# Ending a mixture-of-experts step: the list of further blocks made early, the branches put ahead of the last scatter, and TensorE summing four of nine tiles

## The chip, the cores and the metric

The kernel runs on one core of one Trainium2 chip. Its time is the device time of one execution in microseconds (us). Three runs of the kernel before took 1218.40, 1216.89 and 1221.19 us; the median is 1218.4.

## The reference, cut to what matters

The program is one inference step of a decoder layer with 1024 prompt tokens and 8 sample tokens, 1032 rows of 1024 float32 values in nine tiles: eight of 128 rows, and one of 8. The change touches only the end of the layer, the experts' sum and the final norm:

```python
# each token has one of 4 groups, and in it the best 2 of 8 experts (32 experts in all)
def expert_block(xb, e):
    return (jax.nn.silu(xb @ w_gate[e]) * (xb @ w_up[e])) @ w_down[e]
out = segment_sum(gate_s[:, None] * ybuf[dest], tok_s, num_segments=T)   # two rows a token
h = h + out
y = h * rsqrt(mean(h * h, axis=-1) + EPS) * norm_final
```

So for each token the end computes x + gate0 * y0 + gate1 * y1, and then its RMS norm with the gain.

## The kernel before, in words

Up to the router all goes on as it will after the change: projections, attention, the output projection, the residual sum `xres` in SBUF (nine tiles of 128 x 1024), and the router. The router gives every (token, choice) pair a slot in its expert's block of 96 rows.

**The expert loop** (`for b in range(NE + 1)`, on every engine) runs over 32 experts. SyncE loads 6 MB of weights for each. ScalarE rounds each weight to its upper part (L1316), and VectorE subtracts to get the lower part (L1869, two halves to each of gate, up and down). TensorE makes three products for each pair of tiles (L1032 to L1034, L1063 to L1065). GpSimd fetches the 96 token rows of an expert by an indirect DMA (L1985). It sends the 96 result rows by another (L1990, `send`) to `y_rows` in DRAM: the first choices of all tokens lie in its first half, and the second choices in the other. The result rows have one SBUF buffer, `ysb`, which ScalarE fills (`copy_y`, L1331). Before it fills it for expert b-1, it waits until the rows of expert b-2 are sent (`act.wait_ge(first.sent, 16 * (b - 1))`). The last expert, 31, has its own place for the upper parts of `w_down`.

Experts are taken in such an order that the first choices are complete four experts before the end. So SyncE reads their eight full tiles back while the last experts are computed (`load_y(t, 0, ...)`, L637), and the ninth after the first add.

**The list of further blocks** (`list_further`, L1785 to L1796, VectorE). An expert can have over 96 rows. How many further blocks there are, and of which experts, is worked out from the counts by ten short instructions. With the inputs here there are none. The program must still read the number and branch, on each of the five engines. The list is made after VectorE's last work of the expert loop, and `listed` tells the others.

**The end.** VectorE adds the first choices to all nine tiles (`add_choice(t, 0)`, L1925, nine instructions in a row). Then TensorE, VectorE, ScalarE and GpSimd wait until the last rows are out of their hands: VectorE, ScalarE and GpSimd for all scatters (`first.sent`), TensorE for the last copy. Each reads the number and branches, and GpSimd signals `all_sent`. SyncE waits for `all_sent`, loads the second choices tile by tile (L637), and VectorE does for each tile: the second add (L1925), which ScalarE squares and sums (L1400) and takes the root of (L1403); the reciprocal (L1964); and the closing product (L1967) into one of three output tiles, which SyncE writes out (L685). VectorE's order is add 0, add 1, close 0, add 2, close 1, and so on.

Every engine takes its instructions in order. SyncE's DMAs go in one queue, GpSimd's in another.

## Time and profile before

| what | before |
|---|---|
| median of three runs | 1218.4 us |
| profiled execution | 1217.44 us |
| its span | 1215.4 us |
| TensorE busy | 1148.7 us (95%) |
| VectorE busy | 854.0 us (70%) |
| ScalarE busy | 667.0 us (55%) |
| GpSimd busy | 110.8 us (9%) |
| DMA | 295.12 MB, mean 243 GB/s |

The profile is of one execution. Busy shares are means over the whole span; the change touches its last 50 us and a few microseconds at the start of the expert loop, so the stretches and the chain of waits there say more than the shares. PE is TensorE's products, DVE is VectorE, ACT ScalarE, POOL GpSimd and SP SyncE; SPq is SyncE's queue of DMA issues. The granted TensorE clock of 1.00 is 2.4 GHz, and 0.50 is 1.2 GHz.

### The profile page before, as it was taken

The numbers are of one execution on the slowest core, as the hardware profiler recorded it, in microseconds if no ns is written. First come the engines' busy times: TensorE is split into PE (matmuls) and PEld (weight loads), VectorE is DVE, ScalarE is ACT, GpSimd is POOL, SyncE is SP. The second block draws the span as 40 slices with busy tenths as digits, with TensorE's granted clock in tenths as the row PEclk, the third lists the DMA queues.
The fourth block names the chain that finished last, engine by engine and source line by source line (L and its number), as shares of the span: only waits on it lengthen the run. The fifth ranks groups of instructions, "written<-read, shape, count | busy, mean of one in ns | idle before, by whom it ended". The sixth has DMA issues, their size and how long they took to land.

```text
span 1215.4 us, 17163 instructions
## 1 busy us (share of the span) xinstructions
PE 1148.7 (95%) x6818; PEld 902.1 (74%) x6818; DVE 854.0 (70%) x1213; ACT 667.0 (55%) x831; POOL 110.8 (9%) x130
## 2 busy tenths in 40 slices
PE   7999999999899989999799999999999999999950
PEld 6999999999677747888467777777777777777740
DVE  6315343321677746888788889889888988888877
ACT  7212231111368752332477777777777777777724
POOL 1012210021000000000011111111111111111110
PEclk9999999999999999999899999999999999999985
DMA  8125556141211032111799999999999999999857
GB/s 258 41 80 167 186 185 209 37 138 53 73 51 42 1 132 116 70 70 70 261 395 392 397 395 400 388 388 393 395 389 387 400 387 385 394 395 390 312 215 275
DMA packets 77714, 295.12 MB, mean 243 GB/s; under 512 B 8649, under 2 KB 33353, under 8 KB 52930
## 3 DMA queue, kind: packets, MB, share of 16 engines
q1 hardware_dynamic: 65954, 258.27, 55.6%
q0 software_dynamic: 11680, 35.75, 8.9%
q8 instruction: 55, 0.90, 0.3%
q14 instruction: 25, 0.20, 0.1%
HBM read 268.58 MB, written 33.77 MB: 249 GB/s over the span
## 4 chain that ended last, share of the span: by engine, by line
PE 91%; DVE 3%; ACT 2%; DMA 2%; issue 1%; POOLq 0%; SPq 0%; ACTq 0%; DVEq 0%
PE psum L1034 10%; PE psum L1032 10%; PE psum L1033 10%; PE psum L751 8%; PE psum L753 7%; PE psum L752 7%; PE psum L1063 5%; PE psum L1065 5%; PE psum L1064 5%; PE psum L907 3%; PE psum L829 3%; PE psum L909 3%; PE psum L844 3%; PE psum L908 3%; PE psum L867 2%; PE psum L1022 2%
## 5 line engine op out<-in xcount | busy, mean ns | idle before, releaser
L751 PE MATMUL psum<-h_hi,w_hi 128*128 128x344 f32 x576 | 186.0, 323 | 3.0 <-DVE h_lo L1483 3.0
L753 PE MATMUL psum<-h_hi,w_lo 128*128 128x344 f32 x576 | 184.2, 320 | 0.0
L752 PE MATMUL psum<-h_lo,w_hi 128*128 128x344 f32 x576 | 184.1, 320 | 0.0
L1869 DVE TENSOR_TENSOR w_down_lo<-w_down,w_down_hi 128x2048 fp32r<-128x2048 f32 x62 | 139.4, 2288 | 44.8 <-ACT w_down_hi L1316 44.7
L1869 DVE TENSOR_TENSOR w_gate_lo<-w_gate,w_gate_hi 128x2048 fp32r<-128x2048 f32 x64 | 144.3, 2289 | 23.1 <-ACT w_gate_hi L1316 21.8
L1869 DVE TENSOR_TENSOR w_up_lo<-w_up,w_up_hi 128x2048 fp32r<-128x2048 f32 x64 | 143.7, 2287 | 2.7
L1316 ACT CAST w_gate_hi<-w_gate 128x2048 fp32r<-128x2048 f32 x64 | 119.9, 1915 | 4.4 <-DMA w_gate<-in_w_gate 4.2
L1316 ACT CAST w_up_hi<-w_up 128x2048 fp32r<-128x2048 f32 x64 | 119.3, 1917 | 0.7 <-DMA w_up<-in_w_up 0.6
L1316 ACT CAST w_down_hi<-w_down 128x2048 fp32r<-128x2048 f32 x62 | 115.7, 1907 | 0.7 <-DMA w_down<-in_w_down 0.6
L751 PEld LDWEIGHTS psum<-h_hi,w_hi 128*128 128x128 f32 x576 | 108.3, 188 | 5.4 <-DVE h_lo L1483 3.9
L753 PEld LDWEIGHTS psum<-h_hi,w_lo 128*128 128x128 f32 x576 | 108.4, 188 | 0.0
L752 PEld LDWEIGHTS psum<-h_lo,w_hi 128*128 128x128 f32 x576 | 108.3, 188 | 0.0
L1432 DVE TENSOR_TENSOR w_lo<-w_raw,w_hi 128x1024 fp32r<-128x1024 f32 x23 | 28.1, 1223 | 110.4 <-ACT w_hi L1148 110.4
L1032 PE MATMUL psum<-w_gate_hi,xT_hi 128*96 128x512 f32 x256 | 101.8, 398 | 3.2 <-issue 3.2
L1032 PE MATMUL psum<-w_up_hi,xT_hi 128*96 128x512 f32 x256 | 102.4, 400 | 0.0
L1034 PE MATMUL psum<-w_gate_hi,xT_lo 128*96 128x512 f32 x256 | 101.8, 398 | 0.0
L1033 PE MATMUL psum<-w_gate_lo,xT_hi 128*96 128x512 f32 x256 | 101.4, 396 | 0.0
L1034 PE MATMUL psum<-w_up_hi,xT_lo 128*96 128x512 f32 x256 | 101.1, 395 | 0.0
L1033 PE MATMUL psum<-w_up_lo,xT_hi 128*96 128x512 f32 x256 | 100.7, 393 | 0.0
L1985 POOL DMA_INDIRECT x_rows<-h_rows,gidx x32 | 43.8, 1370 | 612.6 <-DVE gidx L1768 310.1
L1063 PE MATMUL psum<-w_down_hi,hT_hi 128*96 128x512 f32 x248 | 99.4, 401 | 0.0
L1065 PE MATMUL psum<-w_down_hi,hT_lo 128*96 128x512 f32 x248 | 97.7, 394 | 0.0
(252 smaller groups left out, 2065.9 us busy)
## 6 DMA issues: line engine op xcount, KB each, us to landing
w_gate<-in_w_gate SPq DMA_DIRECT2D x64, 1024.0 KB, 15.4
w_up<-in_w_up SPq DMA_DIRECT2D x64, 1024.0 KB, 14.3
w_down<-in_w_down SPq DMA_DIRECT2D x64, 1024.0 KB, 14.1
w_raw<-in_w_in SPq DMA_DIRECT2D x24, 512.0 KB, 4.4
y_tile<-y_rows SPq DMA_DIRECT2D x16, 512.0 KB, 10.4
kv<-in_cache_k POOLq DMA_DIRECT2D x24, 256.0 KB, 4.7
kv<-in_cache_v POOLq DMA_DIRECT2D x24, 256.0 KB, 4.7
x_tile<-in_x_prompt SPq DMA_DIRECT2D x8, 512.0 KB, 4.7
```

Of the source, the lines that this page charges most:

```text
L751: mm(ps[:, 0:TC], wh[:, k, :], h_hi[:, k, cols], start=(k == 0), stop=False)
L752: mm(ps[:, 0:TC], wh[:, k, :], h_lo[:, k, cols], start=False, stop=False)
L753: ins = mm(ps[:, 0:TC], wl[:, k, :], h_hi[:, k, cols], start=False, stop=(k == KD - 1))
L1032: mm(bank(b)[0:SLOTS, :], xT_hi[:, k, :], hi[:, k, :], start=(k == 0), stop=False)
L1033: mm(bank(b)[0:SLOTS, :], xT_hi[:, k, :], lo[:, k, :], start=False, stop=False)
L1034: ins = mm(bank(b)[0:SLOTS, :], xT_lo[:, k, :], hi[:, k, :], start=False, stop=(k == KD - 1))
L1063: mm(out, hT_hi[:, m, :], wd_hi[:, m, cols], start=(m == 0), stop=False)
L1064: mm(out, hT_hi[:, m, :], wd_lo[s][:, m, cols], start=False, stop=False)
L1065: ins = mm(out, hT_lo[:, m, :], wd_hi[:, m, cols], start=False, stop=(m == DE // P - 1))
L1316: nc.scalar.copy(dst[:, part, :], src[:, part, :]).then_inc(ready, 1)
L1869: vec.tensor_tensor(dst[:, part, :], src[:, part, :], hi[:, part, :].bitcast(F32), ALU.subtract).then_inc(split, 1)
L1985: gp.indirect_dma_start(xg, None, h2_d[:, :], bass.IndirectOffsetOnAxis(ap=idx, axis=0)).then_inc(f.rows_in, 16)
```

## The change

**The list** is made after `finish_gates`, ahead of VectorE's loop over the experts. Its small tiles move behind the expert buffers in SBUF. Its two wide intermediates, which had lain in SBUF, now lie in bank 7 of PSUM, and the comparison with 22 block numbers is made in two halves of 11, since a bank holds 512 values in a row. The semaphores `listed` and `early_added` become one, `end_step`: 1 is the list, 2 to 10 are the nine early adds, and 11 to 14 are the four diagonal matrices.

**The branches** of TensorE, ScalarE and VectorE no longer wait for the last scatter or copy ahead of the reading of the number; that wait stands in the branch that is not taken. SyncE now waits for `first.sent` itself and not for GpSimd's `all_sent`. GpSimd keeps its order.

**TensorE's tiles.** For tiles 0 to 3 VectorE makes a 128 x 128 diagonal matrix of the second gates after its early adds. TensorE runs six filler products (`keep_clock`) behind its last expert product. It then multiplies the identity by `xres` of each of the four tiles into two PSUM banks each (eight products), and, when the second choices of a tile have landed, the tile's diagonal by them onto the same banks. `mixed` counts these tiles. ScalarE squares and VectorE closes them from PSUM. Tiles 4 to 8 are added by VectorE as before.

**The order** of the tiles at the end, for the loads, the squares, the closing products and the writes, is 0, 4, 1, 5, 2, 6, 3, 7, 8. VectorE adds tiles 4 and 5 first, then closes tile 0, then 4, adds 6, closes 1 and 5, adds 7, closes 2 and 6, adds 8, and closes 3, 7 and 8.

```diff
@@ -217,11 +217,10 @@
         over = Pack(WEI + 3 * 16384, WEI + 4 * 16384)
-        r_ob, r_inc = (over(f"re{i}", [NE]) for i in range(2))
-        r_mul = over("r_mul", [MORE])
-        r_gt = over("r_gt", [NE, MORE])
-        r_cmp = over("r_cmp", [OVER, NE])
-        r_list = over("r_list", [OVER])
+        listing = Pack(TMP + 16384 + 8 * NE, END)
+        r_ob, r_inc = (listing(f"re{i}", [NE]) for i in range(2))
+        r_mul = listing("r_mul", [MORE])
+        r_list = listing("r_list", [OVER])
         o_mul = over("o_mul", [MORE])
@@ -245,6 +244,9 @@
         gfin = at("gfin", unit(5), [D])
+        MIXED = 4
+        gate_diag = [at(f"gate_diag{k}", unit(5) + 4096 + 4 * P * k, [P]) for k in range(MIXED)]
+        fin_order = [0, 4, 1, 5, 2, 6, 3, 7, 8]
         r_count = at("r_count", TMP + 16384, [NE])
@@ -643,11 +645,11 @@
             sp.dma_start(gfin, a["norm_final"].partition_broadcast(P)).then_inc(gfin_in, 16)
-            sp.wait_ge(early_added, 1)
+            sp.wait_ge(end_step, 2)
             load_y(NY, 0, y_in[0])
-            sp.wait_ge(early_added, NT)
+            sp.wait_ge(end_step, NT + 1)
             sp.wait_ge(first.y_done, NE)
-            sp.wait_ge(listed, 1)
+            sp.wait_ge(end_step, 1)
             more = sp.value_load(oexp[0:1, OVER:OVER + 1], min_val=0, max_val=OVER)
@@ -673,16 +675,16 @@
-            sp.wait_ge(all_sent, 1)
-            for t in range(NY):
+            sp.wait_ge(first.sent, 16 * NE)
+            for t in fin_order[0:NY]:
                 load_y(t, 1, y_in[t])
-            for t in range(NT):
-                if t == 0:
-                    sp.wait_ge(fin_res, 1)
+            for i, t in enumerate(fin_order):
+                if i == 0:
+                    sp.wait_ge(mixed, 1)
                     load_y(NY, 1, y_in[0])
-                sp.wait_ge(fin_out, t + 1)
+                sp.wait_ge(fin_out, i + 1)
                 dst = a["y_prompt"][P * t:P * (t + 1), :] if t < NQ else a["y_sample"]
-                sp.dma_start(dst, ot[t % NO][0:rows(t), :]).then_inc(out_sent[t % NO], 16)
+                sp.dma_start(dst, ot[i % NO][0:rows(t), :]).then_inc(out_sent[i % NO], 16)
             for o in out_sent:
@@ -1088,10 +1090,11 @@
                         down(first, (b - 1) % 2, b - 1, wd_hi_end, hT_hi_end, hT_lo_end)
-            pe.wait_ge(first.y_out, NE)
-            pe.wait_ge(listed, 1)
+            keep_clock(6, bank(0), 512)
+            pe.wait_ge(end_step, 1)
             more = pe.value_load(oexp[0:1, OVER:OVER + 1], min_val=0, max_val=OVER)
             with pe.If(more > 0):
+                pe.wait_ge(first.y_out, NE)
                 place_further()
@@ -1102,6 +1105,20 @@
                     pe.wait_ge(first.y_out, n + 1)
+                pe.wait_ge(back_added, NT)
+            pe.wait_ge(first.y_out, NE)
+            pe.wait_ge(end_step, NT + 1)
+            for k in range(MIXED):
+                for half in range(2):
+                    cols = slice(half * 512, (half + 1) * 512)
+                    mm(bank(2 * k + half), ident, xres[:, k, cols], start=True, stop=False)
+            pe.wait_ge(end_step, NT + 1 + MIXED)
+            for k in range(MIXED):
+                pe.wait_ge(y_in[k], 48 if k == 0 else 32)
+                for half in range(2):
+                    cols = slice(half * 512, (half + 1) * 512)
+                    ins = mm(bank(2 * k + half), gate_diag[k], yt[k][:, cols], start=False, stop=True)
+                ins.then_inc(mixed, 1)
@@ -1376,10 +1393,10 @@
                     upper_down(b)
-            act.wait_ge(first.sent, 16 * NE)
-            act.wait_ge(listed, 1)
+            act.wait_ge(end_step, 1)
             more = act.value_load(oexp[0:1, OVER:OVER + 1], min_val=0, max_val=OVER)
             with act.If(more > 0):
+                act.wait_ge(first.sent, 16 * NE)
                 with act.Fori(0, more, 1) as o:
@@ -1393,13 +1410,18 @@
-            for t in range(NT):
+            for i, t in enumerate(fin_order):
                 w = rows(t)
-                act.wait_ge(fin_res, t + 1)
-                c = t % 2
-                step(nc.scalar.activation(fjunk[0:w, :], xres[0:w, t, :], ACT.Square, accum_out=ssq_f[0:w, c:c + 1]))
-                if t >= 2:
-                    act.wait_ge(fin_out, t - 1)
+                c = i % 2
+                if t < MIXED:
+                    act.wait_ge(mixed, t + 1)
+                    total = bank(2 * t, 2)
+                else:
+                    act.wait_ge(fin_res, t - MIXED + 1)
+                    total = xres[0:w, t, :]
+                step(nc.scalar.activation(fjunk[0:w, :], total, ACT.Square, accum_out=ssq_f[0:w, c:c + 1]))
+                if i >= 2:
+                    act.wait_ge(fin_out, i - 1)
                 nc.scalar.activation(std_f[0:w, c:c + 1], ssq_f[0:w, c:c + 1], ACT.Sqrt, bias=eps[0:w, :],
@@ -1783,17 +1805,21 @@
                 step(vec.tensor_scalar(r_mul, ramp[:, 1:MORE + 1], float(SLOTS), None, ALU.mult))
+                r_gt = bank(7)[:, 0:NE * MORE].rearrange("p (e j) -> p e j", e=NE)
                 step(vec.tensor_tensor(r_gt, r_count.unsqueeze(2).broadcast_to([P, NE, MORE]),
...
                 vec.tensor_copy(oexp[0:1, OVER:OVER + 1], r_inc[0:1, NE - 1:NE])
-                step(vec.tensor_tensor(r_cmp[0:1], r_inc[0:1].unsqueeze(1).broadcast_to([1, OVER, NE]),
-                                       ramp[0:1, 0:OVER].unsqueeze(2).broadcast_to([1, OVER, NE]), ALU.is_le))
-                step(vec.tensor_reduce(r_list[0:1, :], r_cmp[0:1], X, ALU.add))
+                for lo, hi in ((0, OVER // 2), (OVER // 2, OVER)):
+                    n = hi - lo
+                    r_cmp = bank(7)[0:1, 0:n * NE].rearrange("p (o e) -> p o e", o=n)
+                    step(vec.tensor_tensor(r_cmp, r_inc[0:1].unsqueeze(1).broadcast_to([1, n, NE]),
+                                           ramp[0:1, lo:hi].unsqueeze(2).broadcast_to([1, n, NE]), ALU.is_le))
+                    step(vec.tensor_reduce(r_list[0:1, lo:hi], r_cmp, X, ALU.add))
                 step(vec.tensor_scalar(r_list[0:1, :], r_list[0:1, :], float(NE - 1), None, ALU.min))
-                vec.tensor_copy(oexp[0:1, 0:OVER], r_list[0:1, :]).then_inc(listed, 1)
+                vec.tensor_copy(oexp[0:1, 0:OVER], r_list[0:1, :]).then_inc(end_step, 1)
@@ -1899,6 +1925,7 @@
             finish_gates()
+            list_further()
             for b in range(NE + 1):
@@ -1916,8 +1943,6 @@
                     lower_down(first, b % 2, b)
-                if b == NE - 1:
-                    list_further()
@@ -1927,10 +1952,13 @@
                 dve.wait_ge(y_in[t % NY], 16 * (t // NY) + 16)
-                add_choice(t, 0).then_inc(early_added, 1)
-            dve.wait_ge(first.sent, 16 * NE)
+                add_choice(t, 0).then_inc(end_step, 1)
+            for k in range(MIXED):
+                vec.tensor_scalar(gate_diag[k], ident, gates[:, 1, k:k + 1], None, ALU.mult).then_inc(end_step, 1)
+            dve.wait_ge(end_step, 1)
             more = dve.value_load(oexp[0:1, OVER:OVER + 1], min_val=0, max_val=OVER)
             with dve.If(more > 0):
+                dve.wait_ge(first.sent, 16 * NE)
                 table_further()
@@ -1957,23 +1985,26 @@
-            def finish(t):
+            def finish(i):
+                t = fin_order[i]
                 w = rows(t)
-                c = t % 2
-                dve.wait_ge(fin_std, t + 1)
+                c = i % 2
+                total = bank(2 * t, 2) if t < MIXED else xres[0:w, t, :]
+                dve.wait_ge(fin_std, i + 1)
                 step(vec.reciprocal(rst_f[0:w, c:c + 1], std_f[0:w, c:c + 1]))
-                if t >= NO:
-                    dve.wait_ge(out_sent[t % NO], 16 * (t // NO))
-                vec.scalar_tensor_tensor(out=ot[t % NO][0:w, :], in0=xres[0:w, t, :], scalar=rst_f[0:w, c:c + 1],
+                if i >= NO:
+                    dve.wait_ge(out_sent[i % NO], 16 * (i // NO))
+                vec.scalar_tensor_tensor(out=ot[i % NO][0:w, :], in0=total, scalar=rst_f[0:w, c:c + 1],
                                          in1=gfin[0:w, :], op0=ALU.mult, op1=ALU.mult).then_inc(fin_out, 1)
...
-            dve.wait_ge(early_added, NT)
+            dve.wait_ge(end_step, NT + 1)
             dve.wait_ge(gfin_in, 16)
-            add_experts(0)
-            for t in range(NT):
-                if t + 1 < NT:
-                    add_experts(t + 1)
-                finish(t)
+            add_experts(MIXED)
+            add_experts(MIXED + 1)
+            for i, t in enumerate(fin_order):
+                finish(i)
+                if t >= MIXED and t + 2 < NT:
+                    add_experts(t + 2)
@@ -2032,7 +2063,7 @@
             pool.wait_ge(first.sent, 16 * NE)
-            pool.wait_ge(listed, 1)
+            pool.wait_ge(end_step, 1)
             more = pool.value_load(oexp[0:1, OVER:OVER + 1], min_val=0, max_val=OVER)
```

## Rows read from the trace of the kernel before

**Rows 1.** Busy time by stretch: PE, PEld, DVE, ACT, POOL, PEclk, DMA share, GB/s.

```profile
620.00:1150.00 530.00, 530.00 (x2521) 377.75 (x2520) 466.65 (x302) 412.18 (x331) 68.59 (x58) 1.00 1.00 389
1174.00:1184.00 10.00, 0.00 (x0) 0.00 (x0) 5.89 (x5) 1.01 (x1) 3.74 (x2) 0.70 0.10 29
1174.00:1215.40 41.40, 0.00 (x0) 0.00 (x0) 29.11 (x32) 15.17 (x29) 3.74 (x2) 0.55 0.56 211
```

**Rows 2.** Chain of waits at the end: start us, us, what.

```profile
1174.04 1.02 ACT y_rows L1331
...
1175.84 6.31 DMA y_rows<-y_rows,sidx
...
1183.30 4.28 DMA y_tile<-y_rows
...
1192.01 1.28 DVE out_tile L1967
...
1194.60 1.28 DVE out_tile L1967
...
1211.73 1.27 DVE out_tile L1967
```

**Rows 3.** Order of time, ScalarE, first square: start us, us, idle before in brackets.

```profile
1189.02 1.06 ACT L1400 ACTIVATE fjunk<-xres 128x1024 f32<-128x1024 f32 x1 [13.97 <-DVE xres L1925]
```

**Rows 4.** Order of time, VectorE: first experts, a late expert, the end.

```profile
613.73 4.49 DVE L1869 TENSOR_TENSOR w_gate_lo<-w_gate,w_gate_hi 128x2048 fp32r<-128x2048 f32 x2 [4.95 <-ACT w_gate_hi L1316]
...
1107.86 2.29 DVE L1869 TENSOR_TENSOR w_gate_lo<-w_gate,w_gate_hi 128x2048 fp32r<-128x2048 f32 x1 [0.50 <-ACT w_gate_hi L1316]
...
1165.28 0.16 DVE L1785 TENSOR_SCALAR r_mul<-cst 128x10 f32<-128x10 f32 x1
...
1169.06 10.83 DVE L1925 SCALAR_TENSOR_TENSOR xres<-y_tile,gates,xres 128x1024 f32<-128x1024 f32 x9
...
1178.63 1.27 DVE L1925 SCALAR_TENSOR_TENSOR xres<-y_tile,gates,xres 8x1024 f32<-8x1024 f32 x1
```

**Rows 5.** Order of time, TensorE: eight fillers, and the second expert's start.

```profile
590.21 7.11 PE L705 MATMUL psum<-cst 128*128 128x512 f32 x16
...
619.26 0.45 PE L1032 MATMUL psum<-w_gate_hi,xT_hi 128*96 128x512 f32 x1 [1.76 <-issue]
```

**Rows 6.** DMA issues from 1154.76, 1168.90, 1185.69, 1193.32: KB, us to landing.

```profile
y_tile<-y_rows SPq DMA_DIRECT2D x1, 512.0 KB, 14.6
...
y_rows<-y_rows,sidx POOLq DMA_INDIRECT x1, 3.6
...
y_tile<-y_rows SPq DMA_DIRECT2D x1, 512.0 KB, 6.5
...
out_y_prompt<-out_tile SPq DMA_DIRECT2D x1, 512.0 KB, 5.6
```

**Rows 7.** Order of time, SyncE's queue: start us, us of the issue.

```profile
1154.76 0.47 SPq L637 DMA_DIRECT2D y_tile<-y_rows  x1
...
1184.16 1.48 SPq L637 DMA_DIRECT2D y_tile<-y_rows  x1
...
1185.69 0.43 SPq L637 DMA_DIRECT2D y_tile<-y_rows  x1
```

**Rows 8.** Order of time, GpSimd: a late fetch and the last two scatters.

```profile
1109.05 1.89 POOL L1985 DMA_INDIRECT x_rows<-h_rows,gidx  x1 [9.53 <-PE psum L1022]
...
1168.90 0.92 POOL L1990 DMA_INDIRECT y_rows<-y_rows,sidx  x1 [16.29 <-ACT y_rows L1331]
1175.84 3.65 POOL L1990 DMA_INDIRECT y_rows<-y_rows,sidx  x1 [6.02 <-ACT y_rows L1331]
```

**Rows 9.** Order of time, VectorE: SBUF inputs, one PSUM input, one-source pair.

```profile
479.92 0.68 DVE L1589 TENSOR_TENSOR a_lo<-qT,a_hi 128x512 fp32r<-128x512 f32 x1
...
502.30 0.75 DVE L1619 SCALAR_TENSOR_TENSOR xres<-psum,stat,xres 128x512 f32<-128x512 f32 x1 [1.09 <-PE psum L909]
...
514.56 0.57 DVE L1704 TENSOR_SCALAR hot_slot<-cst,r_rank_of 128x96 f32<-128x96 f32 x2
```

More of the change, by code:

```diff
@@ L395, in program @@
         res_out = sem("res_out")
-        listed = sem("listed")
         y_cleared = sem("y_cleared")
-        early_added = sem("early_added")
+        end_step = sem("end_step")
         back_in = sem("back_in")
@@ L402, in program @@
         fin_res = sem("fin_res")
+        mixed = sem("mixed")
         fin_std = sem("fin_std")
```

## The prediction

> **What bounds the kernel now.** I read first the busy time by stretch, to see which stage the change can touch. In the expert loop TensorE is busy all 530 us of the stretch from 620 to 1150 and the clock is at its upper level, 2.4 GHz [rows 1]. Nothing that VectorE, ScalarE or a queue saves there shortens the run, so long as it does not make TensorE wait. From 1174 on TensorE does nothing: in 41 us the end is set by others [rows 1].
>
> Then the chain of waits over these 41 us [rows 2] (a DMA's piece ends at its landing). The last product ends at 1174.0, ScalarE copies it until 1175.06, GpSimd starts the last scatter at 1175.84, it has landed at 1182.15, GpSimd then takes over a microsecond to read the count of further blocks, pass the branch and signal, and SyncE issues the loads of the second-choice rows at 1183.30. The first tile lands at 1187.58. From there the chain is VectorE's: nine adds and nine closing products, until 1213.00. ScalarE's wait before the first square, 14 us, is a wait for this chain and not a bound [rows 3].
>
> Third, VectorE's own order of time around the last experts. The list takes it from 1165.28 to 1169.06, and the nine early adds from 1169.06 to 1179.89, at a pitch of (10.83 - 1.27) / 8 = 1.195 us [rows 4]. None of this is on the path, but it is what GpSimd meets, and this decides the case.
>
> **The list, moved to the start of the experts.** It takes 3.78 us now. The two long instructions of 704 elements become four of 352, and the wide operands lie in PSUM. Four short ones cost what two long ones cost plus two starts, which I put at 0.15 each, and I allow nothing more for PSUM: 4.1 us. VectorE is idle for 4.95 us just there, from 608.78 to 613.73, waiting for ScalarE's first half of the next gate weights [rows 4]. So it is hidden with 0.85 us to spare. The cover is thin, because the split of these weights is followed by that of the token rows, and TensorE sat 1.76 us until 619.26, where those rows are ready [rows 5]: what the list takes over 4.95 us is added to the run. Lower end 0. For the upper end let every one of its wide instructions take twice its time, some 2.6 us more, which gives 1.8 us. I take 0. Behind the last expert VectorE is free 3.78 us earlier, and its adds start at 1165.28. The first-choice tiles are no bar: the last of eight, issued at 1154.76, landed 14.6 us later, at 1169.4, and is used by the eighth add at 1173.6 [rows 6, 7].
>
> **What the earlier adds do to the scatters.** An index row is read from SBUF by GpSimd before it makes the descriptors. In the loop a fetch that was asked for at 1109.05, in the middle of a split by VectorE with both inputs in SBUF, ended at 1110.94, which is 0.79 us after the split's end at 1110.15; a scatter that meets no such work takes 0.92 [rows 4, 8]. The last scatter was asked for at 1175.84, in the sixth early add. It ended at 1179.49, and this is 0.79 us after the end of the eighth add (the ninth started at 1178.63, and two neighbours overlap by 0.07). So it stood through two borders between adds, was let in behind the last add over 128 partitions, and the ninth, over 8 partitions, did not hold it.
>
> The scatter before it, of expert 30, was asked for at 1168.90, while the list's short instructions ran, and took 0.92 [rows 8]. After the change it is asked for at the same time in the fourth of nine adds that follow one another from 1165.28. By the row just read it waits until the eighth add ends, 1165.28 + 7 x 1.195 + 1.27 = 1174.9, and its descriptors are out at 1175.7. It landed 3.6 us after its start, thus 2.7 after its end [rows 6], so now at 1178.4. ScalarE's last copy waits for this landing, since the rows' buffer is single: it starts at 1178.45 instead of 1174.04 and ends at 1179.5. GpSimd starts 0.78 us later as before (1175.06 to 1175.84), at 1180.25, with VectorE idle by then, and the last scatter lands at 1180.25 + 3.6 = 1183.85, against 1182.15. **Term: +1.7 us.**
>
> The Trainium skill, "SBUF — State Buffer", section "Who interferes with whom", says that a VectorE instruction with two SBUF inputs blocks a GpSimd one that reads SBUF, for the whole instruction, and that whichever starts first has the ports. The holding agrees with the trace, the release does not: by that rule the last scatter would have been let in at 1176.3 and not at 1178.70. What the rule would make of the change is the first rival.
>
> **The branch ahead of the last scatter.** SyncE now waits for the scatter itself, with count and branch behind it. GpSimd's 1183.30 - 1182.15 = 1.15 us leave the path [rows 2]; with 0.05 for the wake-up, **-1.1 us**. The loads are issued from 1183.9, and the first tile is there after the same 4.28 us, at 1188.2. The count is read by TensorE, VectorE, ScalarE and SyncE between 1174 and 1178, beside the wait for the scatter. GpSimd's branch comes behind it, where nobody waits for it.
>
> **TensorE's part.** A product of 512 columns in plain float32 took 7.11 / 8 = 0.89 us at the upper clock [rows 5]. Six fillers run from 1174.0 to 1179.3; eight products that bring the four tiles' sums into PSUM follow once the copy has ended, 1179.5 to 1186.6; then it waits for the first tile. Of the 10 us from 1174 the mean grant is 0.70 [rows 1]: 4 us at the upper level and 6 at half, so it held to about 1178, and a wait of 1.6 us should not lower it, and tile 0 is summed at 1188.2 + 1.8 = 1190.0. At half clock it would be 1191.8. ScalarE and VectorE then need 1192.01 - 1189.02 = 3.0 us to the first closing product (square, table load, root, reciprocal) [rows 2, 3]: ready at 1193.0.
>
> But VectorE has two adds in its queue ahead of that product, of tiles 4 and 5. Tile 5 is fourth in the load order. The fourth load was issued at 1185.69 and landed 6.5 us later, at 1192.2, which is 4.6 us behind the first [rows 6, 7]. So now it lands at 1192.8, its add ends at 1194.1, and the first closing product starts at 1194.2 instead of 1192.01. **Term: from the 0.6 us of a later first tile (1.7 - 1.1) to 2.2 us late, +1.6.** It hangs on SyncE's third load, which took 1.48 us to issue where the fourth took 0.43 [rows 7]. If that hitch goes, the term is 1.0 smaller; I keep it, as nothing in the change touches the loads.
>
> **The closing chain.** The pitch of add and product together was 1194.60 - 1192.01 = 2.59 us [rows 2], of the product alone 2.59 - 1.195 = 1.395. From the start of the first product on there were 20.99 us. Now there are five steps without and three with an add, and the last product: 5 x 1.395 + 3 x 2.59 + 1.28 = 16.0. Four products read PSUM instead of SBUF. For 512 columns 0.75 us stand against 0.68 with both inputs in SBUF [rows 9], so 4 x 0.08 = 0.3; lower end 0, upper end 0.6. **Term: 16.3 - 21.0 = -4.7 us.** ScalarE needs some 1.4 us a tile and keeps up. TensorE's tiles 1 to 3 are due long before their turn: even at half clock they would be ready by 1202.6, and the last is wanted at about 1206. Three output buffers: the first write landed 5.6 us after its issue, behind the last load [rows 6]; the fourth product starts 5.4 us after the first one starts, 4.1 after it ends. The last load now lands at 1198.2, and a write queued behind it about 1.3 later, 1199.5; the fourth product is due at 1199.6. It just fits; upper end 1.5 us.
>
> Sum: 1.7 - 1.1 + 1.6 - 4.7 = **-2.5 us**. The profiled execution took 1217.44 us with a span of 1215.4, and it becomes 1214.9. It was 1.0 us below the median of three runs, so for the median 1218.4 - 2.5 = **1215.9 us**. Its own range, by the ends above (hitch gone -1.0, list +1.8, writes +1.5, half clock +0.6, not all together), is 1214.6 to 1217.9.
>
> **Rivals.** (1) The scatter of expert 30 is let in at the next border of adds and lands before 1174. Then the copy stands at 1174.04, the last scatter is asked for at 1175.84, in the ninth add, which ends at 1176.1, is ready at 1176.9 at the latest, and lands at 1179.6. First tile at 1183.9, but TensorE's queue reaches 1186.4 with its fillers and eight products, tile 0 is summed at 1188.2, the first product starts at 1191.2 and the end is 1207.5: -5.5, **1212.9 us**. For it: the page's rule, and the hold over several adds is seen once only. Against it: that one row. (2) The hold lasts until VectorE's queue is empty. Four diagonals, at under 0.3 us each by a pair that took 0.57 [rows 9], follow the adds and end at 1177.3. Then the descriptors are out at 1178.1, the scatter lands at 1180.8, the last one at 1186.25, the first tile at 1190.6; TensorE, idle from 1179.3 to 1181.9 and again before the tile, drops to half clock, tile 0 is summed at 1194.2, the first product is at 1197.2 and the end at 1213.5: +0.5, **1218.9 us**. This is the slower side, and it decides from a release after 1177.4 or so. For it: the hold was over several instructions. Against it: the ninth add let GpSimd in. (3) The list outgrows its gap and TensorE waits at the second expert: -2.5 + 1.8, **1217.7 us**.
>
> **How the numbers follow.** Chances: forecast 0.66, (1) 0.20, (2) 0.08, (3) 0.06. A measurement of this kernel tells 0.3% from no change, which is 3.7 us, so faster means under 1214.7. Of the forecast's 0.66 about 0.11 lies below that (the hitch gone, or the scatter of the runs, 1216.9 to 1221.2), of (1) 0.18: 0.29. Slower, over 1222.1, needs (2) and a mishap more: 0.04. The range runs from (1) to just below (2), 1212.7 to 1218.4.
>
> **What would show it.** In the changed kernel's trace: the scatter of expert 30 lasting some 6.8 us instead of 0.92; ScalarE's last copy starting at its landing and not at the last product's end; the loads issued at the last scatter's landing, without GpSimd's memset between; VectorE waiting for tile 5 ahead of the first closing product; 16.3 us from there to the end. A scatter of expert 30 under 2 us makes me wrong towards (1). A split of the second expert's gate weights that starts later than 613.73 shows (3).

## The result: 6.8 us faster, outside the predicted range

The changed kernel took 1211.07 us (median of 6 runs, 1209.94 to 1214.16), the kernel before, beside it, 1217.88 us (1216.61 to 1222.5). The ratio is 0.9945, with an interval of 0.9926 to 0.9964. The forecast was 1215.9 with a range down to 1212.7: too little gain. The profiled executions are 1217.44 and 1210.50 us, and -6.94 us is what has to be explained.

I cut both at the request of the last scatter and call what follows, until the last closing product ends, the tail. The chain of waits at the end, changed kernel (start us, us, what):

```profile
1173.40 5.15 PE psum L707 x12
1178.55 6.87 PE psum L1114 x16
1185.42 1.73 PE psum L1120 x4
...
1187.17 1.11 ACT fjunk L1422 x2
...
1190.12 1.28 DVE out_tile L1997
...
1204.82 1.27 DVE out_tile L1997
```

The last two scatters, GpSimd's order of time (in brackets the idle time before):

```profile
1168.35 0.91 POOL L2021 DMA_INDIRECT y_rows<-y_rows,sidx  x1 [10.63 <-ACT y_rows L1348]
1175.29 1.16 POOL L2021 DMA_INDIRECT y_rows<-y_rows,sidx  x1 [6.03 <-ACT y_rows L1348]
```

The first load of a second-choice tile, SyncE's queue, and the DMA issue of 1175.29 with its us to landing:

```profile
1179.21 0.34 SPq L639 DMA_DIRECT2D y_tile<-y_rows  x1
```

```profile
y_rows<-y_rows,sidx POOLq DMA_INDIRECT x1, 3.9
```

| stage | before | after | change |
|---|---|---|---|
| until the last scatter's request | 1175.84 | 1175.29 | -0.55 |
| request to the first load's issue | 7.46 | 3.92 | -3.54 |
| issue to the first closing product | 8.71 | 10.91 | +2.20 |
| first closing product to the end of the last | 20.99 | 15.97 | -5.02 |

The sum is -6.91. The tail alone went from 37.17 to 30.80 us. The scatter of expert 30, the hinge of the forecast, took 0.91 and not 6.8 us: the copy was never late. The last scatter took 1.16 instead of 3.65 [rows 8]: it was asked for in the ninth add, the last of the row, and was out 0.87 us after that add's end. The chain before the first closing product changed hands: it is TensorE's queue (fillers until 1178.5, eight products until 1185.4, the sum of tile 0), not SyncE's loads. The busy time by stretch shows it (us, PE, PEld, DVE, ACT, POOL, PEclk, DMA share, GB/s), beside [rows 1]:

```profile
1174.00:1184.00 10.00, 10.00 (x25) 4.40 (x24) 2.49 (x6) 0.50 (x1) 1.25 (x2) 1.00 0.46 159
1184.00:1208.00 24.00, 8.82 (x20) 3.22 (x18) 18.41 (x23) 13.36 (x28) 0.00 (x0) 0.78 0.75 299
```

VectorE, changed kernel, order of time:

```profile
611.72 0.17 DVE L1822 CAST oexp<-r_list 1x22 int32<-1x22 f32 x1
611.81 4.48 DVE L1895 TENSOR_TENSOR w_gate_lo<-w_gate,w_gate_hi 128x2048 fp32r<-128x2048 f32 x2
...
1164.73 10.85 DVE L1950 SCALAR_TENSOR_TENSOR xres<-y_tile,gates,xres 128x1024 f32<-128x1024 f32 x9
...
1168.31 1.29 DVE L1950 SCALAR_TENSOR_TENSOR xres<-y_tile,gates,xres 128x1024 f32<-128x1024 f32 x1
...
1187.11 1.28 DVE L1950 SCALAR_TENSOR_TENSOR xres<-y_tile,gates,xres 128x1024 f32<-128x1024 f32 x1 [1.28 <-DMA y_tile<-y_rows]
1190.12 1.28 DVE L1997 SCALAR_TENSOR_TENSOR out_tile<-psum,stat,gfin 128x1024 f32<-128x1024 f32 x1
1191.51 1.28 DVE L1997 SCALAR_TENSOR_TENSOR out_tile<-xres,stat,gfin 128x1024 f32<-128x1024 f32 x1
```

The reader is to see three things. The fourth early add starts at 1168.31, and the scatter was asked for at 1168.35: 3.62 us after the row of adds began, within 0.04 us of a border between two of them. Tile 5's add started at 1187.11, when its load had landed, and was over 1.7 us before the first product. The last two lines show that a closing product costs 1.28 us from PSUM as from SBUF.

The early list did outgrow its gap in this execution, which is rival 3. It took 4.26 us, from 607.63 to 611.89, where 4.1 had been reckoned. ScalarE had its first half ready at about 608.69 + 1.9 = 610.6, and VectorE started the split at 611.81. TensorE then waited 2.93 us (1.76 before [rows 5]) and ran at half clock for a while:

```profile
608.69 3.70 ACT L1333 CAST w_gate_hi<-w_gate 128x2048 fp32r<-128x2048 f32 x2
```

```profile
617.32 0.71 PE L1034 MATMUL psum<-w_gate_hi,xT_hi 128*96 128x512 f32 x1 [2.93 <-issue]
```

```profile
617.00:620.40 3.40, 3.08 (x8) 2.07 (x9) 3.40 (x4) 3.40 (x3) 0.07 (x1) 0.50 1.00 418
```

The gap itself had shrunk. In the kernel before TensorE ran part of the first expert at half clock (0.51 from 601 to 608 us), in this execution it did not (1.00 there). Two variants of the kernel before that come below, b_shift1 and b_shift3, had 1.00 there as well, and left VectorE 2.90 and 2.87 us where [rows 4] has 4.95:

```profile
612.67 4.49 DVE L1869 TENSOR_TENSOR w_gate_lo<-w_gate,w_gate_hi 128x2048 fp32r<-128x2048 f32 x2 [2.90 <-ACT w_gate_hi L1316]
```

Of the eight profiles with the early list only this one and a_best, both with 1.00 there, overran the gap; the other six had 0.27 to 1.16 us to spare. The stages ahead of the tail move by microseconds from profile to profile: the last scatter was asked for between 1171.85 us (b_shift3) and 1177.63 (b_list_early), a_shift8 aside. So the tail is the sharper measure below, though each is read in a single profile. In the changed kernel and its three shifted variants it came out as 30.8 us four times.

### The profile page after: what moved, and what is told of

Its sections match the earlier page's. It is cut to its first block, busy times and chain, and to the rows that moved or that the text cites. A ratio compares the mean times of both kernels' runs of the same rounds, so it can differ in the third digit from the quotient of the medians.

```text
span 1208.4 us, 17253 instructions
## 1 busy us (share of the span) xinstructions
PE 1168.3 (97%) x6862; PEld 909.2 (75%) x6862; DVE 850.3 (70%) x1215; ACT 666.0 (55%) x831; POOL 112.8 (9%) x130
## 4 chain that ended last, share of the span: by engine, by line
PE 93%; ACT 3%; DVE 2%; issue 1%; DMA 1%; SPq 0%; ACTq 0%; DVEq 0%; POOLq 0%
PE psum L1036 10%; PE psum L1034 10%; PE psum L1035 10%; PE psum L753 8%; PE psum L755 7%; PE psum L754 7%; PE psum L1065 5%; PE psum L1067 5%; PE psum L1066 5%; PE psum L909 3%; PE psum L846 3%; PE psum L831 3%; PE psum L911 3%; PE psum L910 3%; PE psum L869 2%; PE psum L1024 2%
```

## The experiments

Two questions: why was the scatter of expert 30 not held, and what is each part of the change worth? Ratios are to the kernel before, run beside. Where only one execution was made, its time says little: beside b_gaps, b_shift10, a_shift8 and a_shift16 the kernel before was itself executed once, in 1214.77 us, and beside b_shift1, b_shift3 and b_ts2 its median was 1217.2. There the trace is what counts.

**Moving the adds against the scatter.** One to sixteen short stepped instructions go ahead of the row of early adds, in the changed kernel (N = 3, 8, 16) or the kernel before (N = 1, 3, 10):

```
+ for _ in range(N):
+     step(vec.memset(stat[:, 86:87], 0.0))
  for t in range(NT):
      dve.wait_ge(y_in[t % NY], 16 * (t // NY) + 16)
      add_choice(t, 0)...
```

> The changed kernel with three tiny VectorE instructions, each waited for, ahead of the nine early adds, so that the adds start some 0.5 us later. Theory H (hold): a scatter whose index read is asked for inside a row of back-to-back VectorE instructions over 128 partitions with two SBUF inputs waits until the row breaks, and the changed kernel escaped only because the request at 1168.35 fell on the border of the third and fourth add (1168.31). Moved by 0.5 us the request falls inside an add: the scatter of expert 30 lasts some 7 us in place of 0.91, ends 0.8 us after the eighth add, the last scatter lands about 4 us later, the closing chain starts 2 to 2.5 us later: 1213.4 us against 1211.1. Rival Q (the long scatter in the kernel before comes from the queue or the ring of descriptors, not from VectorE's adds): the scatter stays at 0.9 us and the time at 1211.1.

Measured: 1211.82 us (1210.55 to 1212.47), ratio 0.9958 (0.9943 to 0.9973), tail 30.8 us.

```profile
1170.32 1.24 POOL L2023 DMA_INDIRECT y_rows<-y_rows,sidx  x1 [10.10 <-ACT y_rows L1348]
1177.26 1.54 POOL L2023 DMA_INDIRECT y_rows<-y_rows,sidx  x1 [5.70 <-DVE xres L1950]
```

The row of adds began at 1167.10, so the scatter of expert 30 came in the middle of the third add, away from any border, and was out at 1171.56, 0.79 us after that add's end (1167.10 + 2 x 1.195 + 1.27 = 1170.76). It was let in at the next border. So the border at which it fell in the changed kernel was not the whole reason. The tail did not move with the longer scatters: TensorE's queue, which the first closing product waits for, does not depend on them.

> The changed kernel with sixteen tiny VectorE instructions ahead of the early adds, 1.9 us later, so that the scatter of expert 30 is asked for in the second add. Theory E: held until the eighth add ends, 8.8 us. Theory F: 4.0 us. Next border: 1.6 us.

Measured (one execution): 1211.65 us; the scatter of expert 30 in the second add, 1.67 us, the last in the eighth, 1.91 us, both let in at the next border. Tail 30.8 us.

> As a_shift16 with eight, 1.0 us later: the scatter of expert 30 is asked for 0.2 us into the third add. Theory E: 7.9 us. Theory F: 4.3 us. Next border: 1.85 us.

Measured (one execution): 1216.32 us, tail 30.8 us: the loss lies ahead of it. The scatters of experts 29, 30 and 31, and ScalarE's copy for expert 30:

```profile
1151.69 12.51 POOL L2023 DMA_INDIRECT y_rows<-y_rows,sidx  x1 [15.26 <-ACT y_rows L1348]
1171.51 2.00 POOL L2023 DMA_INDIRECT y_rows<-y_rows,sidx  x1 [7.30 <-ACT y_rows L1348]
1181.12 0.91 POOL L2023 DMA_INDIRECT y_rows<-y_rows,sidx  x1 [7.61 <-ACT y_rows L1348]
```

```profile
1169.71 1.01 ACT L1348 COPY y_rows<-psum 96x1024 f32<-96x1024 f32 x1 [5.78 <-DMA y_rows<-y_rows,sidx]
```

What stood in VectorE's queue while the first of them was held ended so:

```profile
1160.51 0.68 DVE L1911 TENSOR_TENSOR hid<-psum,silu_gate 96x512 f32<-96x512 f32 x1
1161.11 2.28 DVE L1895 TENSOR_TENSOR w_down_lo<-w_down,w_down_hi_end 128x2048 fp32r<-128x2048 f32 x1
...
1163.96 0.56 DVE L1915 TENSOR_TENSOR xT_lo<-psum,xT_hi 128x384 fp32r<-128x384 f32 x1 [0.57 <-ACT xT_hi L1343]
```

VectorE ran from split to split with no break until 1163.39, and the scatter was out at 1164.20, 0.8 us later, and landed 18.00 us after its request. It did what I had predicted for expert 30, one expert earlier: the copy waited 5.78 us for its landing and the last scatter was asked for about 5 us late. The adds play no part in this one, and it is not tied to the shift: the scatter of expert 29 took 6.81 and 6.83 us in the two other shifts, 6.71 in a_fill2 and 6.67 in the changed kernel, where the copies were not late. How often the changed kernel meets the long one is not shown. The scatter of expert 30 came in the sixth add here and was let in at the next border.

> The kernel before with ten tiny VectorE instructions ahead of the early adds, which start 1.2 us later. The last scatter is then asked for in the fifth add and not in the sixth, at the same place within it. In three traces so far it was held over two borders and let in ahead of the ninth add, the one over 8 partitions. Theory E (what lets it in is the 8-partition add): it waits three borders and lasts 4.85 us in place of 3.65. Theory F (it stands behind the two adds already in line): 3.65 again, let in ahead of the eighth. The page's rule (next border): 1.3.

Measured (one execution): 1215.68 us, tail 36.6. The last scatter came 0.05 us after the start of the fifth add and took 2.01 us, let in at the next border.

> The kernel before with one tiny VectorE instruction ahead of the early adds (0.16 us later). The last scatter is asked for in the sixth add as in the kernel before. Theory R (which of the adds it is asked in decides): held until ahead of the ninth add, some 3.5 us. Theory M (the tiny instruction ahead of the adds, in whatever way, ends the holding): let in at the next border, 1.2 to 2 us.

Measured (one execution): 1215.92 us, tail 35.2; asked for 5.97 us after the adds' start, which is on a border, and took 0.91. So it decides between neither of the two theories. Here, in b_shift10 and in b_gaps below the tail is not set by the scatter: its chain runs through the end of the adds (1181.21 us here) and SyncE's reading of the count to the first load (1182.59).

> As b_shift1 with three, 0.4 us later; the request still falls in the sixth add. R: some 4.0 us. M: 1.2 to 2 us.

Measured (one execution): 1211.66 us, tail 35.4 (the rest of its distance lies ahead of the tail).

```profile
1171.85 1.66 POOL L1992 DMA_INDIRECT y_rows<-y_rows,sidx  x1 [6.03 <-ACT y_rows L1331]
```

This is 6.39 us after the adds' start, in the sixth add as in the kernel before (6.77), yet it was let in at the next border. Three short instructions ahead of the adds are enough to end the long hold.

**A gap after each add**, kernel before:

```
  add_choice(t, 0).then_inc(early_added, 1)
+ step(vec.memset(stat[:, 86:87], 0.0))
```

> The kernel before with one tiny VectorE instruction, waited for, behind each early add, so that there is a gap between adds. Hold theories E and F alike: the last scatter gets in at the first gap behind the add in which it is asked for, lasts under 2.1 us in place of 3.65, and the tail from its request to the last product is shorter by 1.6 to 2.8 us. If VectorE has nothing to do with the hold, it stays 3.65 us.

Measured (one execution): 1217.64 us, tail 36.1. The last scatter took 0.91. It was asked for 0.07 us after the sixth add's start, just behind a gap:

```profile
1176.55 1.33 DVE L1925 SCALAR_TENSOR_TENSOR xres<-y_tile,gates,xres 128x1024 f32<-128x1024 f32 x1
1176.62 0.91 POOL L1991 DMA_INDIRECT y_rows<-y_rows,sidx  x1 [6.03 <-ACT y_rows L1331]
```

It is inconclusive on the hold over several adds, since it was not held at all; and the gaps make the row of adds longer, until 1181.91, which the loads then wait for.

**Is it the kind of the instruction ahead?** Kernel before, with instructions of another kind:

```
+ for _ in range(2):
+     step(vec.tensor_scalar(r_mul, ramp[:, 1:MORE + 1], float(SLOTS), None, ALU.mult))
```

> The kernel before with two short VectorE multiplications, each waited for, ahead of the early adds: 0.4 us later as with three fills of a cell, which made the hold of the last scatter end at the next border. Theory W (the kind of instruction matters: the fills have no SBUF input, and end a holding that the list's instructions left on): held until ahead of the ninth add, about 4 us. Theory X (where the adds stand in VectorE's instruction stream or its queue decides): next border again, 1.2 to 2 us.

Measured (one execution): 1215.49 us, tail 35.6; asked for 6.38 us after the adds' start, in the sixth, and let in at the next border (1.67 us). Of the two kinds tried, neither leaves the long hold.

**Or is it the wait?** Each of those stepped instructions makes the next one wait. Here the wait alone, for what is already there:

```
+ dve.wait_ge(listed, 1)
  for t in range(NT):
      dve.wait_ge(y_in[t % NY], 16 * (t // NY) + 16)
```

> The kernel before with one wait and no further instruction: VectorE waits for the end of the list's last copy ahead of the first early add, which in the kernel before starts 0.08 us before that copy ends. Theory W (a row of VectorE instructions without any break since the list's copy is what holds GpSimd over several borders; one break ahead of the adds ends it): the last scatter, asked for in the sixth add, gets in at the next border and lasts 1.2 to 2 us in place of 3.65, the tail from its request is 1.6 to 2 us shorter than the 37.2 of the kernel before, and the run some 1.5 us faster. Theory X (an added instruction, that is the place in the stream, did it): 3.65 us and no gain.

Measured: 1215.25 us (12 runs, 1213.85 to 1218.19), ratio 0.9988 (0.9975 to 1.0002), tail 35.9.

```profile
1169.56 0.17 DVE L1796 CAST oexp<-r_list 1x22 int32<-1x22 f32 x1
1169.77 10.84 DVE L1925 SCALAR_TENSOR_TENSOR xres<-y_tile,gates,xres 128x1024 f32<-128x1024 f32 x9
```

```profile
1176.43 1.38 POOL L1991 DMA_INDIRECT y_rows<-y_rows,sidx  x1 [6.02 <-ACT y_rows L1331]
```

With no instruction added, the request 6.66 us after the adds' start came out at the next border (sixth add's end 1169.77 + 5 x 1.195 + 1.27 = 1177.02, plus 0.79 is 1177.81). The adds now start 0.04 us behind the cast's end instead of overlapping it. One wait shortened the scatter from 3.65 to 1.38 us, and the tail by 1.3: the scatter landed 1.65 us sooner after its request (4.66 for 6.31), and the first tile took 0.36 longer to land (4.64 for 4.28). The ratio's interval includes 1, so the runs do not show the gain.

**One part alone, or one part undone.** The list put back behind the last expert, in the changed kernel:

```
  finish_gates()
- list_further()
  ...
+ if b == NE - 1:
+     list_further()
```

> The changed kernel with the list made behind the last expert as before, so that the nine adds start 3.8 us later. Theory H: the scatter of expert 30 meets the list's short instructions and takes 0.9; the last one is asked for inside an add again and is held until the eighth add ends, some 3.5 us in place of 1.16; TensorE's eight products wait for the ninth add. Together about 0.9 us later than the changed kernel, 1212.0. Rival Q: 1211.1, and the last scatter at 0.9 to 1.2 us.

Measured: 1212.18 us (1210.21 to 1212.98), ratio 0.9959 (0.9943 to 0.9974), tail 32.6.

```profile
1169.59 10.83 DVE L1951 SCALAR_TENSOR_TENSOR xres<-y_tile,gates,xres 128x1024 f32<-128x1024 f32 x9
```

```profile
1175.98 4.04 POOL L2022 DMA_INDIRECT y_rows<-y_rows,sidx  x1 [6.03 <-DVE xres L1951]
```

The hold over several adds is back: 6.39 us after the adds' start, out at 1180.02, 0.79 after the eighth add. It is the place of b_shift3's request, without a wait behind the cast. The first closing product came 1.8 us later after the request than in the changed kernel (16.64 for 14.84), and that is the whole of the longer tail.

The list moved, with its wide parts in PSUM as in the changed kernel, and nothing else, in the kernel before:

```
- if b == NE - 1:
-     list_further()
  ...
  finish_gates()
+ list_further()
```

> The kernel before with the list alone moved to the start of the experts (and its wide parts in PSUM). Theory H: the adds start 3.8 us earlier; if the request of the scatter of expert 30 falls on a border of adds as in the changed kernel, the last scatter is no longer held and all behind it is 2.5 us earlier, 1215.4 against 1217.9; if it falls inside an add, it is held for 6 us and the end is 1.7 us later, 1219.6. Rival Q: nothing changes, 1217.9 and a last scatter of 3.6 us.

Measured: 1216.71 us (12 runs), ratio 1.0005 (0.9992 to 1.0019), tail 34.8.

```profile
1167.07 10.85 DVE L1927 SCALAR_TENSOR_TENSOR xres<-y_tile,gates,xres 128x1024 f32<-128x1024 f32 x9
```

```profile
1177.63 1.08 POOL L1992 DMA_INDIRECT y_rows<-y_rows,sidx  x1 [6.03 <-ACT y_rows L1330]
```

The last scatter came in the ninth add and left 2.6 us sooner than before, and the tail is 2.4 us shorter. The median of the runs does not show it. In the profile the request itself came 1.8 us later than in the kernel before (1177.63 for 1175.84); what took the gain in the runs is not settled.

The waits moved into the branches and SyncE waiting for the scatter itself, in the kernel before:

```
- sp.wait_ge(all_sent, 1)
+ sp.wait_ge(first.sent, 16 * NE)
  for t in range(NY):
      load_y(t, 1, y_in[t])
```

> The kernel before with the branches alone put ahead of the last scatter and SyncE waiting for the scatter itself. Both theories: the loads are issued 1.1 us earlier behind the landing, so 1216.8 against 1217.9, the last scatter 3.6 us long as before.

Measured: 1215.27 us (12 runs), ratio 0.9986 (0.9970 to 1.0001), tail 35.2: -1.9, of which 1.15 is GpSimd's branch. The rest is the first tile, which landed 3.46 us after its issue instead of 4.28. SyncE's third load took 0.43 us here and not 1.48; whether the one follows from the other is not shown (b_list_early had 1.36 and 4.03, b_castwait 0.43 and 4.64). The ratio's interval again just includes 1.

```profile
1176.98 3.65 POOL L1991 DMA_INDIRECT y_rows<-y_rows,sidx  x1 [6.02 <-ACT y_rows L1331]
```

The adds began at 1170.21 here, so the request came 6.77 us later and took 3.65, both as in the kernel before to 0.01 us.

**What follows on the hold.** The trace shows when GpSimd's instruction starts and ends; that it is the reading of the index row that is kept out is my reading of it. A held one ended 0.79 us after the end of an add over 128 partitions, or 0.79 to 0.87 after the end of the ninth. Eight requests inside such adds, in seven kernels whose rows of adds began behind a wait (a_shift3, a_shift8, a_shift16 twice, b_shift3, b_shift10, b_ts2, b_castwait), were held to the next border and no further. The three kernels in which the adds ran on behind the list's cast (before, b_branch_ahead, a_list_late) held it to the eighth add's end. In the changed kernel, its variants with fewer fillers and b_list_early the row has no break ahead of it either, but all their requests for expert 30 came at 3.62 us, 0.03 to 0.04 after the start of the fourth add, and got in at once; at 0.05 (b_shift10) and 0.07 (a_shift8) after a start they were held. Their last scatters came in the ninth add, behind which there is no further add to be held by. So no request fell inside the earlier adds of such a row, and whether any unbroken row holds for several borders or only some of them stays open. One sign, no more, is that the three rows with the long hold last 10.83 us and all other unspaced rows 10.84 or 10.85, the changed kernel's among them.

**TensorE's queue.** Fewer fillers, changed kernel, 2 and 0:

```
- keep_clock(6, bank(0), 512)
+ keep_clock(2, bank(0), 512)
```

> The changed kernel with two fillers in place of six. In its trace TensorE's queue is what the first closing product waits for: fillers from 1173.4 to 1178.5, eight products to 1185.4, the first tile's sum to 1187.15, while that tile's rows had landed by 1183.5 or so. With two fillers the eight products start with the ninth add's end, 1175.6, and end at 1182.5; the first sum is ready 1.8 us after the landing, near 1185.3. ScalarE's square, table and root then allow the first closing product at 1188.3, and the add of tile 5, whose rows came at 1187.1, at 1188.5. Theory Q (TensorE's queue binds): the tail is 1.6 us shorter, 1209.4 us against 1211.1. Rival D (the landing of tile 5 and VectorE bind as forecast before the run): no change, 1211.1. If the clock falls in the short wait for the rows, 1.8 us of the gain go.

Measured: 1209.92 us (1209.45 to 1210.72), ratio 0.9922 (0.9894 to 0.9950), tail 30.0. TensorE, then VectorE:

```profile
1176.38 7.11 PE L1114 MATMUL psum<-xres,cst 128*128 128x512 f32 x16 [0.61 <-DVE xres L1950]
1183.89 1.95 PE L1120 MATMUL psum<-y_tile,gate_diag 128*128 128x512 f32 x4 [0.40 <-DMA y_tile<-y_rows]
```

```profile
1188.57 1.28 DVE L1950 SCALAR_TENSOR_TENSOR xres<-y_tile,gates,xres 128x1024 f32<-128x1024 f32 x1 [2.14 <-DMA y_tile<-y_rows]
1189.96 1.28 DVE L1997 SCALAR_TENSOR_TENSOR out_tile<-psum,stat,gfin 128x1024 f32<-128x1024 f32 x1
```

Counted from the last scatter's request, ScalarE starts on tile 0's sum 1.9 us sooner than in the changed kernel (9.94 for 11.88), but the first closing product comes only 0.8 sooner (14.02 for 14.84), because the add of tile 5, queued ahead of it, now waits for its load. That is the wait that I had predicted for the changed kernel itself: it is next in line.

> The changed kernel with no fillers. TensorE then stands still from the last product, 1173.4, to the ninth add's end, 1175.6; the clock before fell 4 us after the end. Expected the same tail as with two fillers, 1209.4; if the clock falls, the products of a tile take 3.6 us in place of 1.8 and the first closing product is 1.8 us later or more, 1211.

Measured: 1209.26 us (1208.36 to 1211.03), ratio 0.9918 (0.9887 to 0.9948), tail 29.6. TensorE stood for 2.32 us and the granted clock stayed at its upper level:

```profile
1174.00:1184.00 10.00, 7.68 (x21) 3.44 (x19) 4.20 (x7) 1.01 (x1) 1.25 (x2) 1.00 0.28 93
```

The fillers gain nothing here: the clock holds without them. The first closing product comes another 1.0 us sooner after the request (12.99), but 0.7 of this is lost further on, where the fourth closing product waits for an output buffer:

```profile
1196.01 1.28 DVE L1996 SCALAR_TENSOR_TENSOR out_tile<-xres,stat,gfin 128x1024 f32<-128x1024 f32 x1 [0.70 <-DMA out_y_prompt<-out_tile]
```

Last, two fillers and tiles 4 and 5 loaded earlier:

```
- for t in fin_order[0:NY]:
+ for t in (0, 4, 5, 1, 2, 6, 3, 7):
      load_y(t, 1, y_in[t])
```

> The changed kernel with two fillers in place of six and the second-choice loads in the order 0, 4, 5, 1, 2, 6, 3, 7, so that VectorE's second add has its rows one load earlier. With two fillers alone the first closing product waited for tile 5, which landed at 1188.5, 8.7 us behind the first issue. As the third load it should land 6.6 to 7.3 us behind it; then ScalarE's root binds, 3.0 us behind tile 0's sum. Expected tail from the last scatter's request 28.9 us against 30.0 with two fillers and 30.8 in the changed kernel: 1208.9 us. If tile 5's landing does not bind, 30.0 and 1209.9.

Measured: 1210.86 us (1208.75 to 1211.97), ratio 0.9948 (0.9933 to 0.9963), tail 29.7. It is no gain over two fillers (30.0). The first closing product comes 1.1 us sooner after the request (12.89), but the closing chain takes 16.84 us instead of 15.97. TensorE waits for tile 1:

```profile
1189.59 6.98 PE L1120 MATMUL psum<-y_tile,gate_diag 128*128 128x512 f32 x12 [2.29 <-DMA y_tile<-y_rows]
```

Tile 1, now fourth in the queue, arrived later, and TensorE resumed at half clock. The chain of waits, though, does not run through TensorE but through the write of the first output tile, for whose buffer the fourth closing product waits:

```profile
1191.61 4.83 DMA out_y_prompt<-out_tile
```

The lowest median is that of the changed kernel without fillers. It is 1.8 us under the changed kernel's, but the two were not run side by side and their intervals overlap: it beats the kernel before, and is not shown to beat the changed one.

## Why the prediction was wrong, point by point

**The step that failed** is "By the row just read it waits until the eighth add ends". It took one row, the 3.65 us of the last scatter, for the rule, and applied it to another scatter in another row of adds. The scatter of expert 30 was let in at once in the changed kernel (0.91 us, not 6.8) and at the next border in a_shift3 and a_shift16 (1.24 and 1.67 us). Two things were wrong. The row of adds before had a peculiarity, which one wait removes (b_castwait); what it is stays open. And the forecast placed the request at 1168.90 and the fourth add's start at 1165.28 + 3 x 1.195 = 1168.87: 0.03 us from a border, where the answer turns over, and I did not say so. That it fell on the border was no merit of the change. The reading that the ninth add, over 8 partitions, holds nothing was wrong too: a request inside it came out 0.79 us after its end (b_list_early, 1.08 us). The +1.7 us was really a gain of 2.4: the last scatter's request came on time, in the last add, and it landed 3.9 us after its request instead of 6.3. These 4.1 us are the error. TensorE's queue took 0.6 of them back, and the 0.55 us ahead of the tail and the 0.3 of the closing chain go on top: together 4.4, from -2.5 to -6.9.

**Rival 1** ("let in at the next border", and landed before 1174) described what happened, at 1212.9 us for the median and 20 in 100, though its rule was not put to the test in the changed kernel, where the request met a border. It gave -5.5 against -6.94 measured. The rest is the stretch ahead of the tail (-0.55, its cause not shown), the 0.3 us for reading PSUM, which cost nothing (1.28 us either way), and the way to the first closing product, fillers, eight products, tile 0's sum and the root, which took about 0.5 less than I reckoned. The rule of the Trainium skill behind it ("SBUF — State Buffer", section "Who interferes with whom": a VectorE instruction with two SBUF inputs blocks GpSimd's access for its own length) holds for the eight requests above and not for the three held over several adds, where 3.65 to 4.04 us were measured, nor for the splits (6.67 and 12.51 us).

**Branch ahead of the scatter**, -1.1: right. GpSimd's 1.15 us are gone, and b_branch_ahead has them in the kernel before.

**Tile 5 before the first closing product**, +1.6: wrong place. TensorE's queue was later than tile 5. The hitch of the third load (1.48 us), which I kept, did not come back (0.43). Tile 5's add was over 1.7 us before the first product; a_fill2 brings the wait out.

**Closing chain**, -4.7: -5.02 measured; the rest is the PSUM term of 0.3, which measured nothing (and which took the difference of a 512-column instruction once for a product of 1024 columns; taken twice it is the 0.6 of its upper end). The chain of products and adds was reckoned rightly. The writes of the output did not hold it here, but "it just fits" was the right warning: with the first closing product 1.8 us sooner they do (a_fill0, 0.70 us).

**List hidden**, 0: rival 3 was seen in the profile of the changed kernel (VectorE 1.2 us late, TensorE waiting 2.93) and in a_best, and in a_shift3 and b_list_early there was room left (0.98 and 0.79 us). The forecast took the gap of 4.95 us for fixed, and it is 2.9 us in executions whose first expert meets no half clock. The price is not separated from the other variation ahead of the tail.

**By parts**, as the tails show them, put in one after the other: the branches take 37.2 to 35.2 (b_branch_ahead), TensorE's part with the new order takes it to 32.6 (a_list_late), and the early list to 30.8, by freeing the last scatter and not by its own 3.8 us. That is -1.9, -2.6 and -1.8. Put into the kernel before alone, the early list is worth -2.4 (b_list_early), so the parts are worth a little more or less by what stands beside them. These are single profiles: of the medians, those of b_list_early and b_branch_ahead cannot be told from the kernel before, and a_list_late's 1212.18 not from the changed kernel's 1211.07. The closing chain alone was 20.99 to 21.00 us in eight profiles with the old order, and 15.97 with the new one wherever no write held it.

## What to carry to other kernels

When one row of a trace carries a forecast, ask how far the two start times are from the border at which the answer changes; if the distance is smaller than the spread between executions, price both answers. A long hold seen once should be taken with what stood around it, here an unbroken run of instructions, and one more wait there took 2.3 us from it. After a chain is shortened, look for the queue that was just behind it: here TensorE's fillers, then a load, then the write of an output tile.

## What the runs showed of the hardware

An indirect DMA's issue on GpSimd can be kept waiting by VectorE for far longer than one instruction. In the changed kernel the scatter of expert 29, harmlessly, took 6.67 us where it had taken 1.01 before:

```profile
1151.05 6.67 POOL L2021 DMA_INDIRECT y_rows<-y_rows,sidx  x1 [15.62 <-ACT y_rows L1348]
```

```profile
1152.42 4.48 DVE L1895 TENSOR_TENSOR w_down_lo<-w_down,w_down_hi 128x2048 fp32r<-128x2048 f32 x2
1156.82 0.55 DVE L1915 TENSOR_TENSOR hT_lo<-psum,hT_hi 128x384 fp32r<-128x384 f32 x1
```

It was out at 1157.72, 0.8 us after the last of the splits (1152.42 + 4.48 = 1156.90): held through several of them and the borders between. The 12.51 us of a_shift8 are the same with a longer unbroken run, which included two instructions with one input in PSUM (0.55 and 0.68 us). The last two scatters, where they met nothing, took 0.91 to 0.92 us, and landed 2.6 to 4.0 us after that. A closing product over 128 x 1024 costs 1.28 us with one input in PSUM, as with both in SBUF. And TensorE kept its upper clock over a stop of 2.32 us (1.00 in the row of a_fill0), while after a stop of 2.29 us in a_best it was granted 0.72 over the 6 us from 1187:

```profile
1187.00:1193.00 6.00, 3.71 (x6) 1.53 (x6) 4.98 (x7) 4.03 (x7) 0.00 (x0) 0.72 1.01 405
```
